# A two-block transformer kernel on one Trainium2 core: modulation of the later layers summed by VectorE inside the feed-forward stages

## What is computed

```python
for l in range(DEPTH_2):                                   # 2 layers
    mod_l = jax.nn.silu(c) @ ada_w[l] + ada_b[l]           # ada_w[l]: 1024 x 9216, for the latents
    mod_c = jax.nn.silu(c_ctx) @ ada_w[l] + ada_b[l]       # the same weights, for the context
    sh1, sc1, g1, sh2, sc2, g2, sh3, sc3, g3 = split(mod_l, 9)
    xl = post_norm(xl, 0.5 * g1 * swiglu(modulate(xl, sh1, sc1), ffn1_w_in[l], ffn1_w_out[l]))   # xc likewise
    yc, yl = even_mixer(...) if l == 0 else odd_mixer(...)  # of modulate(x, sh2, sc2)
    xl = post_norm(xl, g2 * yl)
    xl = post_norm(xl, 0.5 * g3 * swiglu(modulate(xl, sh3, sc3), ffn2_w_in[l], ffn2_w_out[l]))   # xc likewise if l == 0
```

## Time and profile before

| | |
|---|---|
| median of 3 runs | 3052.46 us (3048.05 to 3054.0) |
| the profiled execution | 3042.79 us, its span 3041.0 us |
| mean granted TensorE clock | 0.966 of full speed |
| PE busy, matmuls | 2835.1 us (93%), 17014 |
| VectorE busy | 1264.7 us (42%), 1815 instructions |
| ScalarE busy | 1011.2 us (33%), 1436 |
| POOL busy | 233.2 us (8%), 277 |
| read from HBM | 532.54 MB, 175 GB/s over the span |

### The profile page before, as it was taken

How to read it: one execution, slowest core, us unless ns; L and a number is a source line. 1 busy time by engine, 2 the same in 40 slices (tenths; PEclk the granted TensorE clock), 3 DMA queues, 4 the chain that set the end, 5 groups by cost and what they waited for, 6 DMA issues and landing times.

```text
span 3041.0 us, 39431 instructions
## 1 busy us (share of the span) xinstructions
PE 2835.1 (93%) x17014; PEld 2131.3 (70%) x17014; DVE 1264.7 (42%) x1815; ACT 1011.2 (33%) x1436; POOL 233.2 (8%) x277
## 2 busy tenths in 40 slices
PE   6999899899899889999889989999999999998998
PEld 4854689744434368888667367888878888786998
DVE  4766545511111143333475345333353333435554
ACT  4533444311111142222453224222242222435543
POOL 0025460200000000000030000000000000200000
PEclk8999999899999989999999989999999999999999
DMA  6469756499999942322352542232322323321463
GB/s 245 141 222 332 243 153 180 157 415 421 421 421 421 421 148 87 104 95 84 102 212 68 209 151 70 84 110 87 94 90 87 114 82 98 134 90 42 132 188 97
DMA packets 330186, 536.23 MB, mean 176 GB/s; under 512 B 14324, under 2 KB 291732, under 8 KB 294036
## 3 DMA queue, kind: packets, MB, share of 16 engines
q1 hardware_dynamic: 330004, 533.63, 49.5%
HBM read 532.54 MB, written 1.05 MB: 175 GB/s over the span
## 4 chain that ended last, share of the span: by engine, by line
PE 77%; DMA 12%; DVE 6%; ACT 4%; issue 1%; SPq 0%; POOL 0%; DVEq 0%; ACTq 0%; POOLq 0%
PE ps L186 76%; DMA HF<-in_w_ed 3%; DMA raw_few<-in_w_ed 2%; DMA ALF<-in_w_ed 2%; DMA LF<-in_w_ed 2%; DVE LR L241 1%; DVE ar L241 1%; ACT ar L311 1%; ACT HR L311 1%; DMA RAW<-in_ada_w 1%; DMA RAW<-in_w_ed 1%; PE ps L192 1%; DVE X L241 1%; DMA ALF<-in_w_ada 1%; DVE ar L251 0%
## 5 line engine op out<-in xcount | busy, mean ns | idle before, releaser
L186 PE MATMUL ps<-AH,HR 128*128 128x512 f32 (+1 forms) x2488 | 878.6, 353 | 38.0 <-DVE AL L241 21.9
L186 PE MATMUL ps<-AL,HR 128*128 128x512 f32 (+1 forms) x2488 | 870.8, 350 | 0.0
L186 PE MATMUL ps<-AH,LR 128*128 128x512 f32 (+1 forms) x2488 | 870.4, 350 | 0.0
L241 DVE TENSOR_TENSOR LR<-RAW,HR 128x2048 fp32r<-128x2048 f32 (+3 forms) x232 | 486.7, 2098 | 569.0 <-ACT HR L311 559.4
L311 ACT ACTIVATE HR<-RAW 128x2048 fp32r<-128x2048 f32 (+3 forms) x232 | 404.1, 1743 | 618.1 <-PE ps L186 581.1
L186 PEld LDWEIGHTS ps<-AH,HR 128*128 128x128 f32 x2488 | 480.3, 193 | 108.8 <-ACT ar L311 14.1
L186 PEld LDWEIGHTS ps<-AL,HR 128*128 128x128 f32 x2488 | 480.5, 193 | 58.1
L186 PEld LDWEIGHTS ps<-AH,LR 128*128 128x128 f32 x2488 | 479.4, 193 | 59.5
L241 POOL TENSOR_TENSOR ar<-ar 128x384 f32<-128x384 f32 (+7 forms) x124 | 138.2, 1122 | 1244.6 <-DMA ar<-in_cst 1021.3
L186 PE MATMUL ps<-ar 64*64 64x64 f32 (+8 forms) x1270 | 161.2, 332 | 35.3 <-DVE ar L241 19.8
L251 DVE SCALAR_TENSOR_TENSOR X<-ps,mod,X 128x256 f32<-128x256 f32 x152 | 67.4, 480 | 236.1 <-PE ps L186 236.1
(11 more groups left out here) (220 smaller groups left out, 3414.8 us busy)
## 6 DMA issues: line engine op xcount, KB each, us to landing
RAW<-in_ada_w SPq DMA_DIRECT2D x72, 1024.0 KB, 6.7
RAW<-in_f1i SPq DMA_DIRECT2D x44, 1024.0 KB, 5.1
RAW<-in_f2i SPq DMA_DIRECT2D x44, 1024.0 KB, 5.1
RAW<-in_w_in SPq DMA_DIRECT2D x32, 1024.0 KB, 5.6
RAW<-in_w_ada SPq DMA_DIRECT2D x16, 1024.0 KB, 6.5
RAW<-in_w_eg SPq DMA_DIRECT2D x15, 1024.0 KB, 21.8
HF<-in_w_ed SPq DMA_DIRECT2D x15, 1024.0 KB, 26.7
LF<-in_w_ed SPq DMA_DIRECT2D x15, 1024.0 KB, 24.8
```

What stands on the lines that cost most here:

```text
L186: return self.e.matmul(o, w, x, start=start, stop=stop)
L241: return self.e.tensor_tensor(o, a, b, op) if self.e else NOTHING
```

## The change

`ada2` becomes `lead2`, a job of 8 steps for the first 16 tiles of layer 0 (shift and scale of the first feed-forward stage). With `later` it makes 24 steps, which PE takes one at every place, as before; the table `SPARE` of places holds True everywhere, and `step(True)` takes one step. The 24 are used up in the fifth round of the state-space stage's second group. All `step` and `finish` calls are gone from the gated and the latent attention.

The remaining 56 tiles of layer 0 and the 72 of layer 1 form nine groups, 32 blocks of 512 columns. A block is accumulated by VectorE: `part[v] += w[k] * c[k, v]` over eight row pieces of 128, for both condition vectors (for one in the last eight blocks, where nothing of the context is used any more). Its weights come in two halves of 1 MB that POOL loads into `f.sq`; each half waits until VectorE has used the one before it in the same place. When a block is summed within a partition, PE sums over partitions with `hot`, a matrix of zeros with one column of ones, which also picks the row (8 matmuls of 128 moving columns; 4 for one vector), into bank 0. At the end of a group ScalarE copies the row, PE turns it, VectorE adds the bias. Twelve blocks each are made in `ffns[0]` and `ffns[1]`, eight in `ffns[2]`, none in `ffns[3]`. The feed-forward uses PSUM banks from 1 on while blocks are made.

```diff
+SPARE = [True] * (8 + LAG)
...
-        self.ada2 = [Job("ada_w", i, 0, 72, 2, self.v("ada_b", 72 * i, 72), self.mod2[i], GATES, 3 + 5 * i)
-                     for i in range(2)]
+        self.lead2 = Job("ada_w", 0, 0, 16, 2, self.v("ada_b", 0, 72), self.mod2[0], GATES, 3)
+        self.aside = [self.sem(f"aside{i}") for i in range(2)]
...
-        self.ffns = [Ffn(self, 0, "f1i", "f1o", 0, 512, "lead end", ("evenh", m[0], 24, 512)),
-                     Ffn(self, 0, "f2i", "f2o", 48, 512, "even end", ("f1i1h", m[1], 0, 512)),
-                     Ffn(self, 1, "f1i", "f1o", 0, 512, "f2i0 end", ("oddh", m[1], 24, 512)),
-                     Ffn(self, 1, "f2i", "f2o", 48, 256, "odd end", None)]
...
+        g = Aside.groups((0, 16, 4, 2), (0, 32, 4, 2), (0, 48, 4, 2),
+                         (0, 64, 2, 2), (1, 0, 2, 2), (1, 8, 4, 2), (1, 24, 4, 2),
+                         (1, 40, 4, 1), (1, 56, 4, 1))
+        self.ffns = [Ffn(self, 0, "f1i", "f1o", 0, 512, "lead end", ("evenh", m[0], 24, 512), g[0:3]),
+                     Ffn(self, 0, "f2i", "f2o", 48, 512, "even end", ("f1i1h", m[1], 0, 512), g[3:7]),
+                     Ffn(self, 1, "f1i", "f1o", 0, 512, "f2i0 end", ("oddh", m[1], 24, 512), g[7:9]),
+                     Ffn(self, 1, "f2i", "f2o", 48, 256, "odd end", None, [])]
...
                          o.acs[rows, 256:512], True, True).then_inc(*pe("decay", x))
-            T.step()
+            T.step(SPARE[r])
             if r >= LAG:
...
+def aside_pool(G, K, f):
+
+    for b in f.blocks:
+        g = b.group
+        for h in range(2):
+            c, at = 2 * b.i + h, (g.at + 4 * b.m) * 128
+            if c >= 2 * f.blocks[0].i + 2:
+                G.wait_ge(*K.dve.of("aside chunk", c - 2))
+            src = K.dram["ada_w"][g.layer][512 * h:512 * h + 512, at:at + 512].rearrange("(k p) n -> p k n", p=128)
+            G.dma(f.chunks[h], src).then_inc(K.aside[h], 16)
+
+
+def aside_dve(V, K, f):
+
+    dve = K.dve
+    for b in f.blocks:
+        for k in range(8):
+            h, i = k // 4, 2 * b.i + k // 4
+            w = f.chunks[h][:, k % 4, :]
+            if k % 4 == 0:
+                V.wait_ge(K.aside[h], 16 * (b.i + 1))
+            if k == 0 and b is not f.blocks[0]:
+                V.wait_ge(*K.pe.of("aside", b.i - 1))
+            for v in range(b.group.nv):
+                c, part = K.CS[:, k, 2 + v:3 + v], f.part[:, v, :]
+                if k:
+                    V.wait_ge(*dve.of("aside part", b.i, k - 1, v))
+                    V.stt(part, w, c, part, MUL, ADD).then_inc(*dve("aside part", b.i, k, v))
+                else:
+                    V.ts(part, w, c, None, MUL).then_inc(*dve("aside part", b.i, k, v))
+            if k % 4 == 3:
+                dve.note("aside chunk", i)
+            yield k
...
+def aside_pe(T, K, f, b):
+
+    g = b.group
+    if b.m == 0:
+        row, held = T.hold(0, "aside row", g.i)
+        for h in held:
+            T.wait_ge(*h)
+    T.wait_ge(*K.dve.of("aside part", b.i, 7, g.nv - 1))
+    for v in range(g.nv):
+        for q in range(4):
+            r = T.mm(K.banks[0][32 * q:32 * q + 32, 128 * b.m:128 * b.m + 128], K.hot[:, 1 - v:33 - v],
+                     f.part[:, v, 128 * q:128 * q + 128], v == 0, v == g.nv - 1)
+    r.then_inc(*K.pe("aside", b.i))
+    if b.last:
+        K.pe.note("aside row", g.i)
...
+def aside_turn(T, K, g):
+
+    b, held = T.bank("aside turned", g.i)
+    for h in held:
+        T.wait_ge(*h)
+    T.wait_ge(*K.act.of("aside row", g.i))
+    for m in range(g.count):
+        r = T.mm(b[:, 16 * m:16 * m + 16].rearrange("p (q v) -> p q v", q=4), K.mrow[:, 128 * m:128 * m + 128],
+                 K.ident[:, :].rearrange("p (q c) -> p q c", q=4)[:, :, 0:4], True, True)
+    r.then_inc(*K.pe("aside turned", g.i))
...
+        self.chunks, self.part = [self.sq[:, 4 * i:4 * i + 4, :] for i in range(2)], self.tmp
...
+    def summed(self, *at):
+
+        i = {(0, 2 * p): p - 1 for p in range(1, 6)}
+        i.update({("down", 1): 5, ("down", 5): 6})
+        i.update({(1, 12 + 2 * p): 7 + p for p in range(5)})
+        n = i.get(at, -1)
+        return self.blocks[n] if 0 <= n < len(self.blocks) else None
...
                 r.then_inc(*pe(tag, "up", m0 + i))
+                if i == 0:
+                    aside(p, m0)
...
-                  after=centred_pe(T, K, down, f.X, n, f.sq) if first else None)
+                  after=centred_pe(T, K, down, f.X, n, f.sq) if first else lambda m: aside("down", m))
...
+            if f.done(p, m):
+                aside_act(S, K, f.done(p, m))
...
+            if i and f.turned(p, m - 1):
+                aside_mod(V, K, f.turned(p, m - 1))
+            aside(4)
...
             residual_dve(V, K, down, m, f.X, n, f.gate, [K.act.of(tag + "h", "hi", 7)])
+            if not first:
+                aside((0, 2, 2, 2, 2, 3, 3, 2)[m])
...
     meet(G, K, f.prev)
+    aside_pool(G, K, f)
     K.pool.note(f.tag + " end")
...
-        self.steps = (3, 3, 2, 2, 2, 0, 0)
-        self.pace = (2, 2, 2) + 12 * (1,) + 4 * (0,)
...
         pairs(n, o.F[n % 3][:, 0], o.F[n % 3][:, 1])
-        T.step(o.steps[n])
...
-            T.finish(K.ada2[1])
...
-        T.step(o.pace[n])
```

More of the change, by code:

```diff
@@ L2451, in after_pool, with __init__, groups @@
     K.pool.note("lead end")
+class Block:
+    def __init__(self, i, group, m):
+        self.i, self.group, self.m = i, group, m
+        self.last = m == group.count - 1
+class Aside:
+    def __init__(self, i, layer, at, count, nv, first):
+        self.i, self.layer, self.at, self.count, self.nv = i, layer, at, count, nv
+        self.blocks = [Block(first + m, self, m) for m in range(count)]
+    @staticmethod
+    def groups(*specs):
+        out, first = [], 0
+        for i, (layer, at, count, nv) in enumerate(specs):
+            out.append(Aside(i, layer, at, count, nv, first))
+            first += count
+        return out
@@ new lines, in aside_mod @@
+def aside_mod(V, K, g):
+    bias, dst = K.v("ada_b", 72 * g.layer, 72), K.mod2[g.layer]
+    rows = K.ps("aside turned", g.i)[:, 0:16 * g.count].rearrange("p (t v) -> p t v", v=4)
+    V.wait_ge(*K.pe.of("aside turned", g.i))
+    for t in range(0, 4 * g.count, 8):
+        at = g.at + t
+        V.stt(dst[:, at:at + 8, :], rows[:, t:t + 8, 0:2], GATES.get(at // 8, 1.0),
+              bias[:, at:at + 8].unsqueeze(2).broadcast_to([128, 8, 2]), MUL, ADD).then_inc(*K.dve("aside mod", g.i))
+    K.free(K.dve, "aside turned", g.i)
@@ L2468, in __init__, with done, turned @@
         self.lead = nxt and Lead(*nxt, self.X, self.tmp)
+        self.groups, self.blocks = groups, [b for g in groups for b in g.blocks]
+        self.chunks, self.part = [self.sq[:, 4 * i:4 * i + 4, :] for i in range(2)], self.tmp
         self.passes = ((0, 12, f"{self.tag}d0"), (12, 10, f"{self.tag}d1"))
         ctx.close()
+    def summed(self, *at):
[4 more added lines that the diff above has]
+        return self.blocks[n] if 0 <= n < len(self.blocks) else None
+    def done(self, *at):
+        b = self.summed(*at)
+        return b.group if b and b.last else None
+    def turned(self, *at):
+        before = {(0, 2 * p): (0, 2 * p - 2) for p in range(1, 6)}
+        before.update({("down", 1): (0, 10), ("down", 5): ("down", 1), (1, 12): ("down", 5)})
+        before.update({(1, 12 + 2 * p): (1, 10 + 2 * p) for p in range(1, 5)})
+        before["end"] = (1, 20)
+        return self.done(*before[at if len(at) > 1 else at[0]]) if (at if len(at) > 1 else at[0]) in before else None
 def ffn_pe(T, K, f):
@@ L2475, in ffn_pe, with aside @@
     ready = row_ready(K, tag + "h")
-    for first, cnt, down in f.passes:
+    def aside(*at):
+        if f.turned(*at):
+            aside_turn(T, K, f.turned(*at))
+        if f.summed(*at):
+            aside_pe(T, K, f, f.summed(*at))
+    T.lo = 1 if f.blocks else 0
+    for p, (first, cnt, down) in enumerate(f.passes):
         for m0 in range(first, first + cnt, 2):
@@ L2553, in ffn_dve, with aside @@
     meet(V, K, f.prev)
-    for first, cnt, down in f.passes:
+    parts = aside_dve(V, K, f)
+    def aside(n):
+        for _ in range(n):
+            next(parts, None)
+    for p, (first, cnt, down) in enumerate(f.passes):
         for m in range(first, first + cnt):
@@ L2881, in level @@
             decays(n + 2)
-        S.step(o.steps[n])
     gates("gr", 0)
@@ L2981, in gla_dve @@
         pass
-    V.step(2)
     for m in tiles(V, 8, 1):
@@ L3059, in level @@
                 V.cp(o.far[p][64:128], o.near[p][64:128]).then_inc(*dve("moved", p))
-        V.step(o.steps[n])
     token_rows_dve(V, K, 256)
-    V.step()
     level(0)
```

45 lines of the change are left out of this document (25 added, 20 removed).

## The result

The changed kernel takes **3065.74 us** (median of 7 runs, 3061.25 to 3069.41) against 3051.84 of the kernel before in as many: a ratio of 1.0052, 95% interval 1.0041 to 1.0063. It is slower by 14 us where I forecast 20 us less; the difference is half a per cent, and the interval excludes 1. The profiled execution took 3069.41 us with a span of 3067.2, the one before 3041.0. The two traces differ by 26 us and not by 14, because the profiled execution of before was 9 us faster than its median and that of the change 4 us slower than its own.

A forecast was written before the change was run, and what follows sets the result against it. TensorE (PE) was taken as the bound, holding 77% of the chain of waits. Terms of -6, -19, -26 and +31 us summed to -20, giving 3032 us from the median; range 3016 to 3060, the forecast's own 3018 to 3046.

The forecast's parts named there:

- Rival A: State-space and level rounds: without steps the clock falls to half; sum +14, 3066 us, or 3050 at half price; chance 0.16.
- state-space half: Part of Rival A: at half clock a state-space round costs PE 3.7 us; 20 rounds, +17 us instead of -6.
- the level rounds: Part of Rival A, gated attention: at half clock rounds take 7.8 us instead of 6; six of them, +11 us.
- Term 2: Gated attention: without steps and their loads, earlier starts save 8 us and rounds 13; taken as -19 us.
- term 3: Latent attention: removing steps ahead of and within twelve rounds, and stalls behind them, gives -26 us.
- Term 1: State-space stage: 28 steps removed, rounds then bound by POOL at 2.73 us; -6 us.
- stall of 6.49 us: State-space stage: PE's single wait after the last step, said to move into the second group; costed at nothing.
- The clock falls below 0.9 in the rounds: Sign named in advance that the forecast is wrong: PE's clock below 0.9 in the rounds, where 1.00 was expected.
- Term 4: Feed-forward stages: 32 inserted blocks on PE cost 22.9 us and nine turns 8; +31 us.
- What I cost at nothing on VectorE and POOL: Feed-forward stages: VectorE's 448 operations at 0.69 us and POOL's weight loads fit into slack; no cost.
- rival B: Feed-forward blocks: POOL's transfers land later than 16 us and PE waits; at 18 us +64, 3097 us; chance 0.05.
- Rival C: Attentions: steps only filled waits, so only -18 and -8 are gained against +31; 3057 us; chance 0.12.

The follow-up runs named there:

- e10: Kernel before without layer 1's 36 modulation steps in the gated and latent attention, nothing in their place: ratio 0.9840 to the kernel before, median 3000.2 us.
- e4: Changed kernel with four filler matmuls on constant data wherever the state-space stage has no modulation step left: ratio 1.0034 to the kernel before.
- e5: Changed kernel with hot 64 columns wide, each stage's first two pairs over all eight banks, closing turn in bank 5 or 6: 0.9975, median 3040.7 us.
- e3: Changed kernel with the first two pairs of a feed-forward stage over all eight PSUM banks and the closing turn in bank 0: ratio 1.0036.
- e1: Changed kernel with hot 64 columns wide in place of 33, so BH and BL start at a multiple of 64 bytes: ratio 1.0022.
- e2: Kernel before with an unused 33-column tensor added, so BH and BL start 32 bytes above a multiple of 64: ratio 1.0056.
- e8: Changed kernel keeping VectorE's sums and POOL's loads, but with one small PE matmul per block and no turns, row copies or bias operations: ratio 0.9999.
- e6: As e5, but all 36 steps of layer 0 stay on PE in the state-space stage; only layer 1 goes to VectorE: 0.9888, median 3009.8 us.
- e12: The same kernel as e6, run again: ratio 0.9919 to the kernel before, median 3020.6 us.

## Why the prediction was wrong

- **Direction.** Wrong: 3032 was forecast, 3065.7 measured, above the range of 3016 to 3060. Rival A came near by number (3066), and that is luck: its state-space half came true in part (4 to 14 us where it had 17), its other half, the level rounds, did not, and the feed-forward stages, which it left alone, cost the most.
- **Term 2 and term 3** (gated attention -19, latent attention -26): right, -15.9 and -24.0 in the traces, and -41 in e10, where nothing else was changed.
- **Term 1** (state-space stage -6) failed in the sentence "POOL ends last as soon as the step is gone". POOL does at full clock: 2.76 us a round in e4. But without the steps PE fell to half clock, and then PE ends last with 3.48 us. The stage came out 4 to 14 us longer, depending on the profile. I had put this down as rival A and given it 0.16, with the argument that the trace holds full clock through comparable gaps and that none of mine exceeds 2.5 us. That argument rested on one window of 4 us at 1.00, while the earlier trace rows had level rounds with PE busy 38 of 52 us at 0.89. And the stall of 6.49 us, which I let move in among the rounds without steps and costed at nothing, is longer than 2.5: the half clock of the second group begins in it. I had also written that a busy PE gets the clock back; here it ran without a gap at half clock from 293 to 308 us first. "The clock falls below 0.9 in the rounds" was my own sign of being wrong, and it came. The Trainium skill (TensorE: Matmul & The Clock Gate, "A second HAM failure mode: psum-queue depth-cycling") tells of a clock that oscillates when PE idles briefly and often between groups of matmuls. Here the trace agrees with its direction, 0.57 from 286 to 310 us and 1.00 in the same window with filler; the rule deserved more weight than my counter-example. The level rounds of the gated attention did not go the way of rival A: the stage gained nearly all that was forecast.
- **Term 4** (+31, measured +59) was mis-sized by what it left out, not by its prices: a block cost 0.78 us against 0.77, and e5, with the omissions mended, measured 35, of which 4 are a wait that comes only there. Two causes were not in the sum, and both can be read in the diff:
  - "The feed-forward uses PSUM banks from 1 on" stood in my own description of the change, and I cost it at nothing. Where a stage's first two pairs of tiles are multiplied against rows that arrive one by one, they need eight banks at once. With seven, PE waits 4.06 us for ScalarE's first gate and comes back at a lower clock: 5.9 us in the third stage (e3, e5), about 12 for two. The closing turn in a bank that the down pass needs is 2.2 us and again the clock behind it, 5 to 6 us.
  - The size of `hot` moves every tensor behind it by a number of bytes that is no multiple of 64: 11 us (e1, e2).
- **What I cost at nothing on VectorE and POOL** was right: sums and loads hide (e8), the transfers land in 5.6 us, and rival B did not occur. Rival C did not either.
- **The range** was built from the terms that I had, and omitted terms have no bounds. Banks and address alone are 24 us (the change less e5), more than the forecast gain. It was narrow even so: the bounds of the four terms, added up, reach from 2997 to 3062, and I gave the forecast 3018 to 3046. The sum for rival C also leaves out term 1; with it, it is 3051.

Left open: where the clock falls in the state-space stage differs from run to run (the stage takes 156.6 us in e1 and 167 in e5 and e8, with the same instructions), why the part from the merge to the first feed-forward gate is 4 us shorter in the change, and why the latent attention takes 136 us in e6 and e12, 146 in the change and 149 in e1 and e5.

## What to carry to other kernels

Work that fills the gaps of TensorE in a stage that another engine bounds costs little time there and can keep the clock up (152.6 us for the state-space stage with all steps, 152.1 with filler, 157 to 167 with nothing in their place); look for work to take away where TensorE ends last, and leave it where it doesn't. When a change adds a tensor or takes a bank, list who stands behind it in memory and who rotates over the banks, since the two together cost 24 us here, beside 31 for everything that I had priced. And a small insertion into a full stream costs mostly its switch, so make few and large ones.

## What the runs showed of the hardware

- Products with a moving operand of 128x512 whose tensor begins 32 bytes above a multiple of 64 followed each other in 0.234 us in place of 0.227, 3% slower, in both directions with the same instructions (e1, e2). With 256 columns of the same tensors it was the other way, 0.118 against 0.120. Only this one offset was tried.
- One matmul with 32 columns of weights and 128 moving between products of 128x512 delayed them by 0.54 us (e8), four by 0.56 and eight by 0.78 (the change).
- The state-space rounds without a step fell to half clock behind waits of 1 to 2.5 us in the third group, and of 7.22 us in the second, then took 3.48 us without a gap and stayed there for 20 us and more (the change, e1); with 0.96 us of filler in each, the third group held 1.00 (e4).
